# An encoder trunk on one core: adaLN sums moved to VectorE and TensorE, attention's scaling to ScalarE, the first mixer's end in another order

## The chip, the cores and the metric

The kernel runs on one NeuronCore of a Trainium2 chip. The metric is the device time of one execution in microseconds; the median of three runs stands for the kernel. The core's engines run side by side, each through its own queue in order: TensorE (matmuls and transposes), VectorE (DVE), ScalarE (ACT), GpSimd (POOL) and SyncE (SP), which only issues DMAs. Semaphores order them against each other.

## What is computed

Two layers over x of 1024 tokens by 1024 features, all in f32. Each layer has a token mixer and a gated MLP, each of them modulated by a condition vector c.

```python
def adaln(c, w, b):
    mod = (c @ w + b)[:, None, :]
    shift, scale, gate = jnp.split(mod, 3, axis=-1)
# hybrid_mixer(u): a, g, q, k, v = split(u @ w_in)
    h = a * jax.nn.sigmoid(g)
    h = causal_dwconv(h, conv_w, conv_b)                # 31 taps
    h = jax.nn.silu(layer_norm(h, conv_ln_g, conv_ln_b))
    q, k = partial_rotary(q, cos, sin), partial_rotary(k, cos, sin)
    o = swa_sink_attention(q, k, v, sinks)              # softmax with a sink, window of 2 chunks of 64
    return jnp.concatenate([h, o], axis=-1) @ w_out
# per layer
    u = x * (1.0 + scale) + shift
    x = layer_norm(DN_ALPHA * x + (1.0 + gate) * hybrid_mixer(u), ln1_g, ln1_b)
    # then the same with conv_gated_mlp: (val * silu(dwconv3(gate))) @ w_down
```

## The kernel before

**Slabs.** Features lie on partitions. The work is a list of 128-column weight slabs (`SLABS`), each applied to one of two token blocks of 512. A slab is eight k steps (six or five for the MLP's down projection) of three matmuls, since f32 operands are split into a rounded part and a rest: u_hi with w_hi, u_lo with w_hi, u_hi with w_lo (L727 to L729). A slab's weights are loaded into `raw` by SP four slabs ahead, ScalarE rounds them to w_hi (L916) three slabs ahead, and GpSimd subtracts to get w_lo (L1533, four operations per slab). Slabs 0 to 13 are the first block's w_in (convolution's g and a, then q, k, v), 14 to 21 the second block's q and half of its g and a, 22 to 29 the first block's w_out ("o"), 30 to 35 the rest of the second block's w_in, and from 36 on MLP slabs with the other mixers' slabs between them. Slabs 0 and 1, 22 and 23, 36 and 37 run as pairs. Slab 14 begins at about 131.5 us of the trace, 22 at 206.5 (its first matmul later), 24 at 251.6, 36 at 340.2 and 44 at 402.9.

**The plan.** `plan()` hands the other work to slabs as steps. After its part of slab n (evacuating the slab's bank, splitting weights) each engine does its share of `STEPS[n]`, in order. The steps that matter here: "ad" is a quarter of an adaLN chunk (512 of 3072 columns, eight products of a 128x512 tile with a number of c, two in a quarter), for which SP loads 512 KB, ScalarE multiplies (L1039) and GpSimd adds (L1599, L1603); "as" is the chunk's sum over partitions on TensorE (L824); "fold" adds the biases on VectorE. "tap" is a stretch of the convolution's 31 multiply-adds on VectorE (L1236 to L1246), as many as the slab's budget holds (7.6 each, against `early` for slabs 0 to 21 and `room` after them); "cs" is GpSimd's sum over channels. "ro" and "rs" are the rotation: TensorE permutes (L776), VectorE multiplies and later adds (L1323 to L1338), GpSimd multiplies the other half (L1588, L1590); "vt" turns v.

**Attention** goes by beats, one chunk of 64 tokens each: "sc" scores on TensorE (L796), "mx" maxima on VectorE and exponentials on ScalarE (L1347 to L1352, L1016), "pr" the division by the sum on VectorE (L1357 to L1361), "tr" transposes on TensorE (L805) with a copy on ScalarE (L1025), "pv" the product with v on TensorE (L815), then a_hi on ScalarE (L1031) and a_lo on VectorE (L1369). In slabs 14 to 21 a slab holds sc, pr of the chunk before, mx, tr of two before and pv of three before. Slab 21 is `wait`, the last before w_out: all that is left of the first mixer stands there, first the convolution's mean and centring ("cm", "cc"), then the last beats, then its inverse deviation ("cv", "cq", "cr") and swish ("ck", "cn", "cl").

**The prologue.** VectorE builds the first four adaLN chunks alone (`add_first`, 8 operations for each), TensorE sums them over partitions (L846), then gain and bias are folded and u_hi and u_lo of the first block made. GpSimd computes the rotation's angles and then waits for all 32 additions before it splits the first weights.

**x's normalisation.** "xm", "xc", "xv", "xq", "xr", "xk", "xl" are its mean, centring and squares, inverse deviation, scaling and next inputs; GpSimd sums (L1643, L1614). PSUM banks fg0 to fg2 hold slabs, two in turn before slab 36 and three after it.

## Time and profile before

| what | value |
|---|---|
| median of 3 runs | 2229.36 us (2228.52 to 2230.97) |
| profiled execution | 2230.16 us, span 2228.4 us |
| TensorE matmuls | 2125.2 us busy, 95% of the span |
| VectorE, ScalarE, GpSimd | 1183.0, 1010.4, 1422.8 us busy |

The profile's own two lines of TensorE and of its clock, in 40 slices of the span (busy share and granted clock in tenths, 9 is 90% or more):

```profile
PE   5987898999999999999999999999999999999996
...
PEclk9999889999999999999999999999999999999998
```

The first eighth of the span is where TensorE is not full and where its clock falls. A row of the view of stretches, as used below, holds the stretch and its length, then for TensorE (PE), its weight loads (PEld), VectorE, ScalarE and GpSimd the busy us with the count of instructions, then TensorE's granted clock, the DMA engines' busy share and GB/s. No clock was recorded before 47.9 us; that view counts it as full there.

### The profile page before, as it was taken

The numbers are of one execution on the slowest core, as the hardware profiler recorded it, in microseconds if no ns is written. First come the engines' busy times: TensorE is split into PE (matmuls) and PEld (weight loads), VectorE is DVE, ScalarE is ACT, GpSimd is POOL, SyncE is SP. The second block draws the span as 40 slices with busy tenths as digits, with TensorE's granted clock in tenths as the row PEclk, the third lists the DMA queues.
The fourth block names the chain that finished last, engine by engine and source line by source line (L and its number), as shares of the span: only waits on it lengthen the run. The fifth ranks groups of instructions, "written<-read, shape, count | busy, mean of one in ns | idle before, by whom it ended". The sixth has DMA issues, their size and how long they took to land.

```text
span 2228.4 us, 26925 instructions
## 1 busy us (share of the span) xinstructions
PE 2125.2 (95%) x9491; PEld 1719.5 (77%) x9491; DVE 1183.0 (53%) x1916; ACT 1010.4 (45%) x1760; POOL 1422.8 (64%) x1786
## 2 busy tenths in 40 slices
PE   5987898999999999999999999999999999999996
PEld 4865676787888877878778888888778888888885
DVE  6767766666522545567762365467763254332224
ACT  2645444554532656436352565424353364433332
POOL 5886585676566887767556876555555767545452
PEclk9999889999999999999999999999999999999998
DMA  8644342343343334534323432332323333334332
GB/s 281 183 115 123 87 131 85 106 143 101 109 119 104 117 111 141 158 114 136 98 75 104 127 99 82 104 90 79 93 78 98 96 89 92 116 93 135 88 95 73
DMA packets 417283, 248.79 MB, mean 112 GB/s; under 512 B 44309, under 2 KB 389245, under 8 KB 417149
## 3 DMA queue, kind: packets, MB, share of 16 engines
q1 hardware_dynamic: 416282, 246.72, 37.6%
q8 instruction: 76, 1.25, 0.2%
q14 instruction: 58, 0.48, 0.1%
q10 hardware_dynamic: 867, 0.35, 0.1%
HBM read 242.77 MB, written 4.26 MB: 111 GB/s over the span
## 4 chain that ended last, share of the span: by engine, by line
PE 72%; POOL 15%; issue 6%; DVE 4%; ACT 2%; DMA 1%; SPq 1%; DVEq 0%; POOLq 0%; ACTq 0%
PE fg L727 23%; PE fg L729 23%; PE fg L728 23%; POOL w_lo L1533 8%; POOL ada_acc L1603 3%; PE bank_s L796 1%; POOL q L1588 1%; DVE bank_c L1241 1%; POOL ssum L1643 1%; POOL ssum L1614 1%; PE bank_t L815 1%; DMA first_ada<-in_w_ada_mix_dram 1%; PE bank_l L734 0%; PE bank_t L805 0%; POOL ada_acc L1599 0%
## 5 line engine op out<-in xcount | busy, mean ns | idle before, releaser
L1533 POOL TENSOR_TENSOR w_lo<-raw,w_hi 128x256 fp32r<-128x256 f32 (+1 forms) x1440 | 1036.0, 751 | 721.8 <-ACT w_hi L916 717.8
L727 PE MATMUL fg<-u_hi,w_hi 128*128 128x512 f32 x2112 | 853.7, 404 | 8.6 <-DVE u_lo L1290 4.4
L728 PE MATMUL fg<-u_lo,w_hi 128*128 128x512 f32 x2112 | 828.6, 392 | 0.0
L729 PE MATMUL fg<-u_hi,w_lo 128*128 128x512 f32 x2112 | 827.9, 392 | 0.0
L916 ACT ACTIVATE w_hi<-raw 128x1024 fp32r<-128x1024 f32 (+2 forms) x392 | 379.4, 968 | 411.0 <-PE fg L729 332.9
L727 PEld LDWEIGHTS fg<-u_hi,w_hi 128*128 128x128 f32 x2112 | 400.8, 190 | 109.3 <-issue 23.6
L728 PEld LDWEIGHTS fg<-u_lo,w_hi 128*128 128x128 f32 x2112 | 401.0, 190 | 89.9 <-issue 9.7
L729 PEld LDWEIGHTS fg<-u_hi,w_lo 128*128 128x128 f32 x2112 | 400.4, 190 | 85.8
L1455 DVE SCALAR_TENSOR_TENSOR x<-fg,mod,x 128x512 f32<-128x512 f32 x160 | 120.0, 750 | 373.1 <-PE fg L729 373.1
L1241 DVE SCALAR_TENSOR_TENSOR bank_c<-glu,par,bank_c 128x512 f32<-128x512 f32 x448 | 305.5, 747 | 0.0
L727 PE MATMUL fg<-h_hi,w_hi 128*128 128x512 f32 x704 | 281.3, 400 | 1.7 <-DVE h_lo L1488 1.7
L728 PE MATMUL fg<-h_lo,w_hi 128*128 128x512 f32 x704 | 278.4, 395 | 0.0
L729 PE MATMUL fg<-h_hi,w_lo 128*128 128x512 f32 x704 | 278.4, 395 | 0.0
L1465 DVE SCALAR_TENSOR_TENSOR fg<-gate,par,fg 128x512 f32<-128x512 f32 x88 | 66.5, 755 | 362.8 <-ACT fg L1100 362.7
L1603 POOL TENSOR_TENSOR ada_acc<-ada_acc,ada 128x512 f32<-128x512 f32 x120 | 156.4, 1304 | 5.9 <-ACT ada L1039 1.1
L727 PEld LDWEIGHTS fg<-h_hi,w_hi 128*128 128x128 f32 x704 | 132.3, 188 | 34.1 <-DVE h_lo L1488 2.1
L728 PEld LDWEIGHTS fg<-h_lo,w_hi 128*128 128x128 f32 x704 | 132.3, 188 | 32.0 <-issue 1.0
L729 PEld LDWEIGHTS fg<-h_hi,w_lo 128*128 128x128 f32 x704 | 132.3, 188 | 32.0
L1110 ACT ACTIVATE h_hi<-fg 128x512 fp32r<-128x512 f32 x88 | 52.6, 598 | 198.6 <-DVE fg L1481 198.6
L1039 ACT ACTIVATE ada<-ada,ccol 128x512 f32<-128x512 f32 x160 | 106.3, 715 | 12.4 <-DMA ada<-in_w_ada_ffn_dram 12.3
L1481 DVE SCALAR_TENSOR_TENSOR fg<-fg,tanh_c 128x512 f32<-128x512 f32 x88 | 61.4, 698 | 61.7 <-PE fg L729 60.1
L1105 ACT ACTIVATE tanh_c<-fg 128x512 f32<-128x512 f32 x88 | 52.7, 599 | 70.3 <-DVE fg L1468 70.3
(209 smaller groups left out, 1759.4 us busy)
## 6 DMA issues: line engine op xcount, KB each, us to landing
raw<-in_w_up_dram SPq DMA_DIRECT2D x176, 512.0 KB, 3.8
ada<-in_w_ada_ffn_dram SPq DMA_DIRECT2D x48, 512.0 KB, 4.4
raw<-in_w_down_dram SPq DMA_DIRECT2D x64, 384.0 KB, 3.4
raw<-in_w_in_dram SPq DMA_DIRECT2D x40, 512.0 KB, 3.9
raw<-in_w_down_dram SPq DMA_DIRECT2D x64, 320.0 KB, 3.0
ada<-in_w_ada_mix_dram SPq DMA_DIRECT2D x32, 512.0 KB, 4.6
first_ada<-in_w_ada_mix_dram SPq DMA_DIRECT2D x8, 1024.0 KB, 12.6
raw<-in_w_in_dram SPq DMA_DIRECT2D x32, 256.0 KB, 3.7
```

The lines of the kernel that those rows point to most:

```text
L727: pe.matmul(out[:], hi[:, k, :], rhi, start=k == order[0], stop=False)
L728: pe.matmul(out[:], hi[:, k, :], rlo, start=False, stop=False)
L729: ins = pe.matmul(out[:], lo[:, k, :], rhi, start=False, stop=k == order[-1])
L916: act.activation(w_hi[n % NHI][:, 0:nk, :], raw[n % NRAW][:, 0:nk, :], ACT.Copy).then_inc(hi_ready, 1)
L1039: act.activation(ada[m % 2][:, i, :], ada[m % 2][:, i, :], ACT.Copy, scale=ccol[:, k:k + 1]).then_inc(ada_mul, 1)
L1105: act.activation(tanh_c[:], ps[:], ACT.Tanh, scale=0.5).then_inc(gate_act, 1)
L1241: ins = dve.scalar_tensor_tensor(out=conv[:, j, :] if k == CONV_K - 1 else acc[:], in0=src, scalar=w, in1=acc[:], op0=ALU.mult, op1=ALU.add)
L1455: dve.scalar_tensor_tensor(out=xs(b, k), in0=ps[:], scalar=at_gate, in1=xs(b, k), op0=ALU.mult, op1=ALU.add).then_inc(freed["dve"], 1)
L1465: dve.scalar_tensor_tensor(out=ps[:], in0=gate[:, 1:1 + T], scalar=par3[:, l, i + FT:i + FT + 1], in1=ps[:], op0=ALU.mult, op1=ALU.add).th ...
L1481: dve.scalar_tensor_tensor(out=ps[:], in0=ps[:], scalar=0.5, in1=tanh_c[:], op0=ALU.mult, op1=ALU.mult).then_inc(gate_dve, 1)
L1533: ins = pool.tensor_tensor(w_lo[n % NRAW][:, ks, :], raw[n % NRAW][:, ks, :], w_hi[n % NHI][:, ks, :].bitcast(F32), ALU.subtract)
L1603: pool.tensor_tensor(acc[:], acc[:], rows[:, i, :], ALU.add).then_inc(ada_add, 1)
```

## The change

1. `add_first` makes six instead of eight operations per chunk (`ADDED_FIRST`). TensorE multiplies the columns of k = 6 and 7 itself, accumulating in the same bank, and then adds the sums of VectorE's part. The weights of slab 1 are loaded before the last two adaLN loads, and GpSimd no longer waits for the additions before it splits the first weights.
2. Chunks 8, 9 and 10 (`DVE_CHUNKS`) are multiplied and added on VectorE, two operations per quarter; ScalarE and GpSimd leave them out. Chunks 5 to 12 stand beside other slabs than before, none of them beside the two first rotations (slabs 9 to 13 and 37 to 41). Two folds of gates and one of gain and bias move five to seven slabs back.
3. "pr" keeps its two small operations on VectorE; the product with the reciprocals goes to ScalarE as four activations of 128 columns. Its budget falls from 11 to 3.
4. In slabs before 21 VectorE does "pv" after the taps. The budget of slabs 14 to 21 rises from 75 to 80. In the planner's count the first mixer's taps then end in slab 19, its mean and centring stand in slab 20 (`middle`), and in slab 21 the last beats are interleaved with the inverse deviation.
5. GpSimd does its half of the rotation ahead of w_lo in each slab.

```diff
@@ -104,6 +104,7 @@
+LAST_BEAT = POS["o", 0, 0, 0] - 1
...
@@ -155,9 +160,9 @@
-    fixed = {"ro": 14, "mx": 13, "pr": 11, "pv": 5, "cc": 7, "cq": 36, "ck": 7, "cn": 7, "cl": 7, "xc": 7, "xq": 36, "xk": 7,
+    fixed = {"ro": 14, "mx": 13, "pr": 3, "pv": 5, "cc": 7, "cq": 36, "ck": 7, "cn": 7, "cl": 7, "xc": 7, "xq": 36, "xk": 7,
              "xl": 7, "il": 0, "xt": 7, "fold": 8, "hist": 0}
-    early = [62] * 5 + [58] * 4 + [64] * 5 + [75] * (POS["o", 0, 0, 0] - 14)
+    early = [62] * 5 + [58] * 4 + [64] * 5 + [80] * (POS["o", 0, 0, 0] - 14)
@@ -242,14 +247,16 @@
-    quarters = {4: 2, 5: 6, 6: 10, 7: 14, 8: 18, 9: 22, 10: 26, 11: (32, 33, 36, 37), 12: 44, 13: 56, 14: 60, 15: 80, 16: 106,
-                17: 124, 18: 128, 19: 140, 20: 144, 21: 154, 22: 158, 23: 204}
+    quarters = {4: 2, 5: (6, 7, 8, 14), 6: 15, 7: 19, 8: 23, 9: 27, 10: (31, 32, 34, 35), 11: 42, 12: 48, 13: 56, 14: 60, 15: 80,
+                16: 106, 17: 124, 18: 128, 19: 140, 20: 144, 21: 154, 22: 158, 23: 204}
...
+            if c in DVE_CHUNKS:
+                used[n] += 15
         put(ns[-1] + 2, "as", c)
-    for n, what, i in ((12, "gate", 0), (28, "ss", 1), (40, "gate", 1), (100, "ss", 2), (145, "gate", 2), (165, "ss", 3),
+    for n, what, i in ((18, "gate", 0), (33, "ss", 1), (47, "gate", 1), (100, "ss", 2), (145, "gate", 2), (165, "ss", 3),
@@ -273,16 +280,26 @@
-    taps(0, 1, wait)
-    beat(wait, wait - first)
-    put(wait, "cm", 0)
-    for k in range(CT):
-        put(wait, "cc", 0, k)
-    for i in range(wait - first + 1, NCH + 3):
-        beat(wait, i)
-    conv_norm_rest = ("cv", "cq", "cr")
-    for what in conv_norm_rest:
-        put(wait, what, 0)
+    end = taps(0, 1, wait)
+    i = wait - first
+    middle = min(end + 1, wait)
+
+    def norm_first():
+        put(middle, "cm", 0)
+        for k in range(CT):
+            put(middle, "cc", 0, k)
+
+    if middle < wait:
+        norm_first()
+    chunk_step(wait, 0, ("sc", i), ("pr", i - 1), ("mx", i))
+    if middle == wait:
+        norm_first()
+    chunk_step(wait, 0, ("tr", i - 2), ("pv", i - 3))
+    put(wait, "cv", 0)
+    put(wait, "cq", 0)
+    chunk_step(wait, 0, ("tr", i - 1), ("pv", i - 2), ("pr", i))
+    put(wait, "cr", 0)
+    chunk_step(wait, 0, ("tr", i), ("pv", i - 1), ("pv", i))
...
@@ -589,7 +606,7 @@
                 if m >= 2:
-                    sp.wait_ge(ada_add, added(m - 2))
+                    sp.wait_ge(ada_add[added(m - 2)[0]], added(m - 2)[1])
@@ -631,9 +648,9 @@
+            load_w(1)
             load_first(6)
             load_first(7)
-            load_w(1)
@@ -817,7 +834,8 @@
             def sum_ada(c):
-                pe.wait_ge(ada_add, 7 * (c - CHUNKS_BEFORE + 1))
+                e, adds = added((c - CHUNKS_BEFORE + 1) * QUARTERS - 1)
+                pe.wait_ge(ada_add[e], adds)
@@ -840,10 +858,16 @@
+            pe.wait_ge(set_col, 1)
             for c in range(CHUNKS_BEFORE):
-                pe.wait_ge(first_add, DT * (c + 1))
+                pe.wait_ge(in_first[2 * c + 1], 16)
+                for k in range(ADDED_FIRST, DT):
+                    for i in range(TB):
+                        pe.matmul(bank_s[:, c * TB + i:c * TB + i + 1], first_ada[2 * c + 1][:, k % (DT // 2), i * P:(i + 1) * P],
+                                  ccol[:, k:k + 1], start=(c, k, i) == (0, ADDED_FIRST, 0), stop=False)
+                pe.wait_ge(first_add, ADDED_FIRST * (c + 1))
                 for i in range(c * TB, (c + 1) * TB):
-                    ins = pe.matmul(bank_s[:, i:i + 1], first_acc[:, i * P:(i + 1) * P], ones_1[:, 0:1], start=True, stop=True)
+                    ins = pe.matmul(bank_s[:, i:i + 1], first_acc[:, i * P:(i + 1) * P], ones_1[:, 0:1], start=False, stop=i == 2 * DT - 1)
@@ -1016,6 +1040,13 @@
+            def normalise(mi, i):
+                n, r = NCH * mi + i, i % 2
+                act.wait_ge(att_pr, 3 * n + 2)
+                for p in range(QT):
+                    ins = act.activation(probs[:, r, p, :], probs[:, r, p, :], ACT.Copy, scale=st[:, r, 6, p:p + 1])
+                ins.then_inc(att_pr, 1)
@@ -1129,11 +1160,13 @@
+                    elif what == "pr":
+                        normalise(*step[1:])
...
-                    elif what == "ad":
+                    elif what == "ad" and step[1] not in DVE_CHUNKS:
...
@@ -1268,6 +1301,21 @@
+            def add_ada(c, part):
+                m = (c - CHUNKS_BEFORE) * QUARTERS + part
+                rows, acc, n = ada[m % 2], ada_acc[c % 2], added(m)[1]
+                dve.wait_ge(in_ada[m % 2], 16 * (m // 2 + 1))
+                for i in (0, 1):
+                    weight = ccol[:, 2 * part + i:2 * part + i + 1]
+                    if part == 0 and i == 0:
+                        if c >= CHUNKS_BEFORE + 2:
+                            dve.wait_ge(ada_sum, c - CHUNKS_BEFORE)
+                        dve.tensor_scalar(acc[:], rows[:, 0, :], weight, None, ALU.mult).then_inc(ada_add["dve"], 1)
+                    else:
+                        dve.wait_ge(ada_add["dve"], n - 2 + i)
+                        dve.scalar_tensor_tensor(out=acc[:], in0=rows[:, i, :], scalar=weight, in1=acc[:],
+                                                 op0=ALU.mult, op1=ALU.add).then_inc(ada_add["dve"], 1)
@@ -1351,16 +1399,12 @@
-            def normalise(mi, i):
+            def weights(mi, i):
...
-                dve.wait_ge(att_pr, 3 * n + 2)
-                dve.tensor_tensor(probs[:, r, :, :], probs[:, r, :, :],
-                                  st[:, r, 6, :].rearrange("p (i o) -> p i o", o=1).to_broadcast([P, QT, P]),
-                                  ALU.mult).then_inc(att_pr, 1)
...
@@ -1417,7 +1463,7 @@
             for c in range(CHUNKS_BEFORE):
-                for k in range(DT):
+                for k in range(ADDED_FIRST):
@@ -1435,7 +1481,9 @@
-                mine = [step for step in STEPS[n] if step[0] in DVE_STEPS]
+                mine = [step for step in STEPS[n] if step[0] in DVE_STEPS or step[0] == "ad" and step[1] in DVE_CHUNKS]
+                if n < LAST_BEAT:
+                    mine.sort(key=lambda step: step[0] == "pv")
@@ -1592,15 +1640,16 @@
-                pool.wait_ge(ada_mul, 2 * (m + 1))
+                n = added(m)[1]
+                pool.wait_ge(ada_mul, 2 * sum(added(i)[0] == "pool" for i in range(m + 1)))
...
-                    pool.tensor_tensor(acc[:], rows[:, 0, :], rows[:, 1, :], ALU.add).then_inc(ada_add, 1)
+                    pool.tensor_tensor(acc[:], rows[:, 0, :], rows[:, 1, :], ALU.add).then_inc(ada_add["pool"], 1)
                 else:
                     for i in (0, 1):
-                        pool.wait_ge(ada_add, added(m - 1) + i)
-                        pool.tensor_tensor(acc[:], acc[:], rows[:, i, :], ALU.add).then_inc(ada_add, 1)
+                        pool.wait_ge(ada_add["pool"], n - 2 + i)
+                        pool.tensor_tensor(acc[:], acc[:], rows[:, i, :], ALU.add).then_inc(ada_add["pool"], 1)
@@ -1643,9 +1692,9 @@
-            pool.wait_ge(first_add, DT * CHUNKS_BEFORE)
             for n in range(2):
                 split_lo(n)
+            pool.wait_ge(ada_sum, 1)
@@ -1653,6 +1702,9 @@
             for n in range(NSLAB):
+                for step in STEPS[n]:
+                    if step[0] == "ro":
+                        rope(*step[1:])
@@ -1663,9 +1715,7 @@
-                    elif what == "ro":
-                        rope(*step[1:])
-                    elif what == "ad":
+                    elif what == "ad" and step[1] not in DVE_CHUNKS:
@@ -1679,7 +1729,9 @@
 def added(m):
-    return 7 * (m // QUARTERS) + 2 * (m % QUARTERS) + 1
+    engines = ["dve" if CHUNKS_BEFORE + i // QUARTERS in DVE_CHUNKS else "pool" for i in range(m + 1)]
+    e = engines[m]
+    return e, sum(2 - (e == "pool" and i % QUARTERS == 0) for i in range(m + 1) if engines[i] == e)
```

## Rows read from the trace of the kernel before

**Rows 1.** The view of stretches, five between slab boundaries.

```profile
131.50:206.50 75.00, 61.80 (x311) 49.92 (x310) 57.80 (x100) 35.24 (x96) 53.48 (x59) 0.93 0.43 127
206.50:251.60 45.10, 25.97 (x98) 17.23 (x98) 27.03 (x57) 19.38 (x47) 11.27 (x12) 0.70 0.09 24
251.60:340.20 88.60, 78.34 (x326) 62.68 (x324) 63.86 (x102) 44.39 (x65) 77.17 (x86) 0.91 0.49 143
340.20:402.90 62.70, 56.66 (x218) 43.93 (x218) 36.04 (x55) 23.66 (x38) 34.91 (x43) 0.88 0.26 76
402.90:2228.40 1825.50, 1798.84 (x8083) 1460.33 (x8081) 907.71 (x1473) 823.30 (x1419) 1150.46 (x1461) 0.99 0.36 105
```

**Rows 2.** Stretches again: slab 25 (plain), slab 28 and slab 31.

```profile
257.98:263.42 5.44, 5.44 (x25) 4.50 (x24) 5.12 (x8) 3.16 (x5) 5.36 (x6) 1.00 0.67 194
274.30:286.40 12.10, 9.73 (x34) 7.98 (x34) 4.05 (x6) 3.78 (x6) 12.02 (x14) 0.72 0.51 146
297.27:307.44 10.17, 8.18 (x27) 6.13 (x27) 6.08 (x10) 3.93 (x6) 9.29 (x11) 0.83 0.29 93
```

**Rows 3.** TensorE's waits, 44 to 405 us: releaser, us in total, times, longest.

```profile
PE bank_t L786 <- DVE kz L1338: 13.0, 2, 8.4
...
PE bank_l L734 <- POOL ssum L1631: 5.3, 1, 5.3
...
PE bank_l L824 <- POOL ada_acc L1603: 2.7, 2, 2.4
```

**Rows 4.** Timeline of the prologue: start, us, instruction, idle before and its releaser.

```profile
31.51 5.54 DVE L1173 SCALAR_TENSOR_TENSOR first_acc<-first_ada,ccol,first_acc 128x512 f32<-128x512 f32 x7
...
35.22 1.06 ACT L916 ACTIVATE w_hi<-raw 128x1024 fp32r<-128x1024 f32 x1 [8.97 <-DMA raw<-in_w_in_dram]
...
37.11 1.86 PE L846 MATMUL bank_s<-const,first_acc 128*128 128x1 f32 x8 [4.17 <-DVE first_acc L1173]
37.19 6.51 POOL L1533 TENSOR_TENSOR w_lo<-raw,w_hi 128x256 fp32r<-128x256 f32 x8 [3.12 <-issue]
...
41.04 1.21 DVE L1221 TENSOR_TENSOR u_lo<-tmp,u_hi 128x512 fp32r<-128x512 f32 x1
```

**Rows 5.** Timeline at the first mixer's end, VectorE and TensorE.

```profile
214.54 0.68 DVE L1444 SCALAR_TENSOR_TENSOR glu<-tanh_c,fg 128x512 f32<-128x512 f32 x1
...
239.32 1.28 DVE L1303 TENSOR_TENSOR conv<-conv,bank_l 128x512 f32<-128x512 f32 x2 [2.17 <-PE bank_l L742]
...
251.59 0.94 PE L824 MATMUL bank_l<-const,ada_acc 128*128 128x1 f32 x8
```

**Rows 6.** Timeline of TensorE at the first rotation's last two steps.

```profile
134.14 1.10 PE L776 MATMUL bank_t<-probs,const 128*128 128x512 f32 x2 [2.47 <-DVE q L1333]
...
149.24 1.09 PE L786 MATMUL bank_t<-const,v_t 128*128 128x128 f32 x4 [8.38 <-DVE kz L1338]
```

**Rows 7.** Groups of GpSimd's instructions, 252 to 300 us: busy us, mean ns, idle.

```profile
L1533 POOL TENSOR_TENSOR w_lo<-raw,w_hi 128x256 fp32r<-128x256 f32 x32 | 22.6, 743 | 23.5 <-ACT w_hi L916 23.5
L1603 POOL TENSOR_TENSOR ada_acc<-ada_acc,ada 128x512 f32<-128x512 f32 x11 | 14.3, 1296 | 0.4
```

**Rows 8.** Groups of VectorE's instructions, 150 to 207 us (beats of slabs 14 to 21).

```profile
L1241 DVE SCALAR_TENSOR_TENSOR bank_c<-glu,par,bank_c 128x512 f32<-128x512 f32 x34 | 22.9, 747 | 0.0
L1361 DVE TENSOR_TENSOR probs<-probs,st 128x512 f32<-128x512 f32 x6 | 6.2, 1038 | 0.2
...
L1369 DVE TENSOR_TENSOR u_lo<-fg,u_hi 128x256 fp32r<-128x256 f32 x3 | 1.3, 425 | 7.3 <-ACT u_hi L1031 7.3
```

**Rows 9.** Timeline of VectorE: two small operations of one beat.

```profile
161.28 0.17 DVE L1349 SCALAR_TENSOR_TENSOR st<-st,nsink 128x4 f32<-128x4 f32 x1
161.49 0.67 DVE L1352 TENSOR_TENSOR st<-st,nsink 128x4 f32<-128x4 f32 x1
```

**Rows 10.** Timeline of one attention beat of the second mixer, ScalarE and TensorE.

```profile
487.23 0.60 ACT L1110 ACTIVATE h_hi<-fg 128x512 fp32r<-128x512 f32 x1 [1.84 <-DVE fg L1481]
...
487.19 0.60 PE L805 MATMUL bank_t<-const,probs 128*128 128x128 f32 x4
```

12 lines of the change are left out of this document (8 added, 4 removed).

## The prediction

> **What bounds the kernel now.** I read the busy table first. TensorE is busy for 2125.2 of 2228.4 us, so 103 us are idle, and the clock line falls in a few slices of the first fifth and in the last. Next I read the stretches, cut at slab boundaries. From 402.9 us on TensorE is busy 1798.8 of 1825.5 us at a granted clock of 0.99, while each of the four stretches before it loses idle time and clock together [rows 1]. Whatever this change wins must come from the first 403 us. One k step of a slab is three matmuls and a slab of eight steps (24 matmuls) takes 5.44 us at the full clock [rows 2]. That is the floor against which I measure each stretch. The list of waits then names who ends the idle time: the keys of the rotation, and GpSimd's sums for the convolution and for adaLN [rows 3].
>
> **Part 1, first adaLN sums.** VectorE makes six of eight additions per chunk; TensorE takes the products for k = 6 and 7 and later adds the column sums. Now the last seven additions run from 31.51 to 37.05 us with no wait, the four sums follow until 38.97, and the first slab starts at 43.91, as GpSimd's w_lo (eight operations, 6.5 us) is done at 43.7 and had sat idle for 3.1 us until VectorE's last addition [rows 4]. After the change GpSimd doesn't wait: it is free at 34.1, so w_lo is ready near 40.6. The load of slab 1's weights moves ahead of the last two adaLN loads. ScalarE's split of those weights shows their landing, 35.2 [rows 4]; as the same bytes are moved in another order, I take 35.2 for the last adaLN load instead. VectorE needs two more additions (0.79 apart), to 36.8. TensorE needs eight more matmuls of a 128-column weight, 16 records. Eight such records take 1.86 us at the 1.2 GHz level [rows 4], so 16 take 3.7, and with the final 1.9 the sums end at 40.8, 1.8 later than now; at the 2.4 GHz level eight take 0.94 [rows 5], and the end is 38.0, 1.0 earlier. The first u_lo ends 42.2 at most, 3.3 or less after the sums [rows 4], which gives 41 to 44. Near the middle that is 1.4 earlier, and u_lo no longer shares its time with w_lo: I take 2 us saved, with bounds from 4 saved to 1.5 lost.
>
> **Part 2, slabs 14 to 21 (131.5 to 206.5 us, 75.0 us).** Two waits of 2.5 and 8.4 us stand here [rows 6]. Both are GpSimd's half of the rotation: its queue ran late, since each slab cost 3.0 (w_lo, four operations) + 2.6 (adaLN) [rows 7] and two more operations of 128x512 at 1.3 us, for the rotation and the second block's u_lo: 8.2, more than a slab. Now no adaLN part stands beside slabs 9 to 13 and the rotation goes ahead of w_lo: 5.6 us per slab, below the 6.0 of a slab with its rotation (5.44 and 0.5 [rows 2, 6]). The keys then come from VectorE, which has up to 6 additions of the convolution ahead of them (0.67 each [rows 8]), 7 to 9 us after slab 13's end at 131.5, where now TensorE goes on 17.7 after it. Slab 14 ends some 6.4 after slab 13, so 0.5 to 2 us of wait stay. TensorE's own work in the stretch is 61.8 us [rows 1]; 1.9 of it is the half clock that the long wait brings, the convolution's mean adds 1.1 to it, and with 2 of wait that is 63, so 12 saved. Eight slabs in it make a beat of 7.6 us, and this holds if VectorE keeps that pace. Its work in a beat: glu 0.7 (half of them), maxima 1.4, reciprocal 0.4, a_lo 0.4, six or seven additions at 0.67, in all 7.0. The product with the reciprocals (1.04 each) leaves for ScalarE, and the wait for a_hi (7.3 us in three beats) is now behind the additions [rows 8]. ScalarE pays four activations of 128 columns, about 0.27 apart as its exponentials are, 1.1 us, and is busy under half of this stretch [rows 1]. Bounds: 9 to 14 saved.
>
> **Part 3, the end of the first mixer (206.5 to 251.6, 45.1 us).** I follow the chain. VectorE reaches glu of slab 21 only at 214.54, 8.0 us after the slab [rows 5]; with a pace of 7.0 that lag goes. The convolution's additions end in slab 19, so its mean, centring (2.5) and squares run beside slab 21, and the 5.3 us wait for GpSimd's sum [rows 3] goes too. The rest, from slab 21's end: glu and reciprocals 1.2, maxima to 3.0, exponentials to 4.7, t_copy and a_hi to 5.7, a_lo to 6.1, inverse root and diagonals to 9.9, a_lo and reciprocals to 10.7, the weights' scaling on ScalarE to 11.9, transposes and product with v for the last two chunks, with their copies, to 16.5. From there the swish chain is unchanged: from 239.32 to the pair's end at 251.6 is 12 [rows 5]. That is 28.3 us, 17 saved. What is late next is the same alternation of VectorE and ScalarE; nothing else ends later. Bounds: 10 (a lag of half a beat stays and ScalarE's new step sits in the chain twice) to 20.
>
> **Part 4, slabs 24 to 35 (88.6 us).** Twelve slabs are 65.3. GpSimd pays 3.0 for w_lo, 1.3 for the residual sum and 2.6 for adaLN, 6.9 a slab and above 5.44 [rows 7], and TensorE waits for its adaLN sum (2.7 in all [rows 3]) and later for its residual sum; the clock falls each time (0.91 [rows 1]). With chunks 8 to 10 on VectorE, GpSimd has 4.3. Slab 28 with its wait takes 12.1 and slab 31 takes 10.2 [rows 2]; a plain slab with the small matmuls before it is 6.3, so 5.8 and 3.9 can go. The square sums before slab 33 alternate with ScalarE and stay. VectorE takes two additions per part, 1.5 us; with 0.75 for x and three convolution additions (2.0) an output slab holds 4.3. Two things cost: the fold for the second modulation moves from slab 28 to 33, in front of the normalisation's scaling (5 small operations of 0.17 to 0.67 us [rows 9], 0.9 to 3.4, minus about 1 beside TensorE's broadcast), and part 2 of chunk 10 stands in the middle of that scaling (1.5). I take 1.7 lost for both, since VectorE's other operations there run freer: 8 saved. Bounds 3 to 11. Each load of a part is queued on SP behind the weights; it lands 4 to 6 us later. VectorE would wait for it with the next x update behind it, but the banks of an output slab are needed only a slab later, so I cost that at nothing; without that cover it is 2 to 5 us once, after slab 23.
>
> A rule speaks against this part. Small VectorE operations with both inputs in SBUF take 0.17 us at one time and 0.67 right after [rows 9], when GpSimd is busy, while the convolution's additions, one of whose inputs is in PSUM, stay at 0.747 [rows 8]. The Trainium skill ("SBUF — State Buffer", Who interferes with whom) says that a VectorE instruction with two SBUF inputs locks GpSimd's reads out for its length. The new additions are of that kind. By that rule 24 of them could each hold GpSimd for 0.75 us, 18 us of its time over 13 slabs; with it GpSimd has 4.3 + 1.4, 0.3 above a slab, some 3 us late by the end and within the low bound.
>
> **Part 5, slabs 36 to 43 (62.7 us).** The wait for the keys comes again, 13.0 - 8.4 = 4.6 us [rows 3, 6], and the queries' sums are late before it; TensorE is busy 56.7 of 62.7 us, of which about 3.2 are lost to the clock (0.88) [rows 1]. With the rotation ahead of w_lo, which here waits for ScalarE, and chunk 11 moved to slabs 42 to 45, GpSimd's half is done 2.2 us after the rotation. The floor is 56.7 - 3.2 = 53.5. Saved 9, bounds 5 to 11.
>
> **Part 6, from 402.9 us.** One adaLN sum of 0.8 moves into this stretch. In the attention beats of mixers 1 to 3 the scaling sits on ScalarE ahead of a_hi. Now ScalarE is idle for 1.84 us behind a_hi, until 487.2, which is when the transposes that need a_hi's bank start, at 487.19 [rows 10]. With 1.1 us more, a_lo is done near 487.0: just in time in beats with an adaLN part. Mixer 1's additions end four slabs later (they yield to the adaLN parts), so its normalisation falls on three more beats. I take 2 us lost, bounds from 1 gained to 8 lost.
>
> **Sum.** 2 + 12 + 17 + 8 + 9 - 2 = 46. The profiled execution took 2230.2 us (span 2228.4, 1.8 around it), which gives 2184.2; the median of the runs is 2229.4, 0.8 below it, so the forecast is 2183.4.
>
> **The rivals.** (a) VectorE stays the bound in slabs 14 to 21: small operations at 0.67 beside GpSimd and seven additions instead of six make a beat of 8.5 or more. For it: the beats now lengthen from 7.6 to 10. Against it: 1.04 plus 2.4 of waiting leave every beat. Then part 2 gives 8, part 3 gives 8, the rest stays: 46 - 13 = 33, 2196; with part 4 at its low end, 28, 2201. (b) More than forecast: the waits' end keeps the clock at 2.4 GHz throughout the four stretches, and the sums of the prologue run at it. Lost to clock now in 131.5 to 402.9: roughly 0.07x75, 0.09x89 and 0.12x63, 21 us, of which I have counted about 9; so up to 12 more, 2171. By the Trainium skill ("TensorE: Matmul & The Clock Gate", What's actually happening) activity releases the throttle; the trace agrees, as the clock falls only around the waits named. (c) Slower than before: ScalarE, with 1.1 us more, becomes late in every one of the 24 attention beats of mixers 1 to 3, so that the transposes wait for bank_t. Place: the second slab of each pair. It tells from the first delay beyond the slack of [rows 10]; to cancel 46 us each beat must lose 1.9, and at 2.4 the time is 2241. Against it: ScalarE is 45% busy there. (d) The change does nothing where the idle time is, because another wait takes over in each stretch (the loads, for one): 2229.
>
> **Chances.** Forecast 0.70, with its own range 2174 to 2197; (a) 0.14; (b) 0.11; (c) 0.03; (d) 0.02. The range 2170 to 2202 takes in (a) and (b) and leaves out part of the tails of each, (c) and (d). A measurement of this kernel tells 0.2%, 4.5 us, from no change: faster 0.95, same 0.02, slower 0.03.
>
> **What would show it.** Right: in the list of waits the keys (13.0) fall below 3, GpSimd's adaLN sum and the convolution sum vanish, slab 21 ends near 192, the output pair near 220, and the stretch from slab 44 on keeps its 1825 us within 3. Part 1 is wrong if the first slab starts after 43.9; part 2 if VectorE's glu of slab 21 comes more than 2 us after the slab; part 3 if the pair's end is over 33 us after slab 21; part 4 if VectorE sits idle for adaLN loads with TensorE waiting behind it. The prediction as a whole is wrong if the attention beats after 403 us show waits for ScalarE over 10 us, or if the clock still falls in as many places as now.

## The result, and the profile after

| what | before | after |
|---|---|---|
| median (lowest to highest of 4) | 2229.47 us (2228.52 to 2230.97) | 2189.45 us (2187.96 to 2193.33) |
| ratio, 95% interval | 1 | 0.9822 (0.981 to 0.9834) |
| profiled execution | 2230.16, span 2228.4 | 2193.33, span 2190.8 |

The change saves 40.0 us, 1.8%, against a forecast of 46. The profiled execution of after is the longest of its four, 3.9 above the median, so its stretches add up to 37.6 saved. Below, single stretches are compared in profiles and totals by medians; where the two disagree, the text gives both. The page's two lines of TensorE after:

```profile
PE   7998989999999999999999999999999999999996
...
PEclk9998989999999999999999999999999999999998
```

The view of stretches, at the same slab boundaries as [rows 1] (columns as there):

```profile
131.58:196.62 65.04, 62.36 (x313) 49.66 (x312) 56.80 (x98) 44.69 (x133) 44.64 (x52) 0.97 0.43 130
196.62:228.76 32.14, 23.42 (x95) 15.65 (x93) 17.04 (x41) 17.62 (x42) 7.78 (x8) 0.73 0.11 33
228.76:312.69 83.93, 74.90 (x326) 60.70 (x325) 69.12 (x107) 32.67 (x47) 64.92 (x70) 0.94 0.55 169
312.69:364.59 51.90, 51.58 (x218) 40.71 (x219) 35.53 (x55) 22.44 (x36) 30.84 (x39) 0.97 0.28 82
364.59:2190.80 1826.21, 1798.69 (x8091) 1460.41 (x8089) 891.55 (x1469) 853.91 (x1522) 1148.11 (x1469) 1.00 0.36 106
```

| stretch | before | after | saved | forecast |
|---|---|---|---|---|
| to slab 13's end | 131.5 | 131.6 | -0.1 | 2 |
| slabs 14 to 21 | 75.0 | 65.0 | 10.0 | 12 |
| end of the first mixer | 45.1 | 32.1 | 13.0 | 17 |
| slabs 24 to 35 | 88.6 | 83.9 | 4.7 | 8 |
| slabs 36 to 43 | 62.7 | 51.9 | 10.8 | 9 |
| the rest | 1825.5 | 1826.2 | -0.7 | -2 |

TensorE's waits after, 44 to 400 us (releaser, us in total, times, longest):

```profile
PE fg L744 <- DVE u_lo L1338: 5.4, 1, 5.4
PE fg L832 <- DVE u_lo L1413: 3.5, 2, 1.9
PE bank_l L759 <- DVE diag L1302: 3.1, 1, 3.1
PE bank_l L755 <- POOL ssum L1663: 2.8, 1, 2.8
...
PE bank_l L755 <- POOL ssum L1670: 0.8, 1, 0.8
PE bank_t L803 <- ACT q L1111: 0.7, 1, 0.7
```

Against [rows 3], the keys (13.0) and the adaLN sums (2.7) are gone and the convolution's sum is down from 5.3 to 0.8. Most of what is left belongs to two chains that no step of the change shortens: inverse root and diagonals at the mixer's end (3.1; before 3.6 in two waits), and x's normalisation before slabs 33 (2.8; before 1.3) and 36 (5.4; before 4.4). The wait of 1.9 in the second line is new. Slab 21 ends at 196.6 and the pair at 228.8, where I had 192 and 220.

The prologue after, as a timeline:

```profile
31.84 7.93 POOL L1581 TENSOR_TENSOR w_lo<-raw,w_hi 128x256 fp32r<-128x256 f32 x8
...
37.05 3.57 PE L866 MATMUL bank_s<-ccol,first_ada 128*128 128x1 f32 x16 [1.43 <-DMA first_ada<-in_w_ada_mix_dram]
40.48 1.84 PE L870 MATMUL bank_s<-const,first_acc 128*128 128x1 f32 x8
...
44.11 0.67 DVE L1254 TENSOR_TENSOR u_lo<-tmp,u_hi 128x512 fp32r<-128x512 f32 x1
...
44.93 0.76 PE L744 MATMUL fg<-u_hi,w_hi 128*128 128x512 f32 x1 [1.86 <-DVE u_lo L1254]
```

GpSimd is early, as forecast, and u_lo takes 0.67 instead of the 1.21 of [rows 4]. But the last adaLN load lands at 37.05, and TensorE's products and sums stand behind it: the first slab starts at 44.93, 1.0 later than before. By slab 13's end all but 0.1 of that is made up.

### The profile page after: what moved, and what is told of

It is laid out like the page before. It is cut to its first block, busy times and chain, and to the rows that moved or that the text cites. A ratio compares the mean times of both kernels' runs of the same rounds, so it can differ in the third digit from the quotient of the medians.

```text
span 2190.8 us, 27121 instructions
## 1 busy us (share of the span) xinstructions
PE 2127.2 (97%) x9555; PEld 1725.9 (79%) x9555; DVE 1161.0 (53%) x1900; ACT 1031.0 (47%) x1864; POOL 1391.3 (64%) x1765
## 3 DMA queue, kind: packets, MB, share of 16 engines
q8 instruction: 76, 1.25, 0.2%
## 4 chain that ended last, share of the span: by engine, by line
PE 83%; POOL 5%; DVE 4%; ACT 3%; issue 3%; SPq 1%; DMA 1%; DVEq 0%; POOLq 0%; ACTq 0%
PE fg L744 26%; PE fg L746 26%; PE fg L745 26%; POOL w_lo L1581 2%; DVE bank_c L1274 1%; PE bank_s L813 1%; POOL ssum L1663 1%; POOL ada_acc L1652 1%; ACT ada L1070 1%; DMA first_ada<-in_w_ada_mix_dram 1%; PE bank_t L832 1%; SPq L602 1%; PE bank_t L793 0%; PE bank_l L842 0%; PE bank_l L751 0%
## 5 line engine op out<-in xcount | busy, mean ns | idle before, releaser
L1652 POOL TENSOR_TENSOR ada_acc<-ada_acc,ada 128x512 f32<-128x512 f32 x102 | 132.2, 1296 | 4.5 <-ACT ada L1070 0.5
L1070 ACT ACTIVATE ada<-ada,ccol 128x512 f32<-128x512 f32 x136 | 90.3, 714 | 3.6 <-DMA ada<-in_w_ada_mix_dram 2.6
```

The lines of the kernel that those rows point to most:

```text
L1070: act.activation(ada[m % 2][:, i, :], ada[m % 2][:, i, :], ACT.Copy, scale=ccol[:, k:k + 1]).then_inc(ada_mul, 1)
L1652: pool.tensor_tensor(acc[:], acc[:], rows[:, i, :], ALU.add).then_inc(ada_add["pool"], 1)
```

## The experiments

All are edits of the changed kernel ("after"), with its stretches as the yardstick: first slab at 44.9, then 65.0, 32.1, 83.9 and 51.9 us. How far a stretch moves by itself can be read where an edit doesn't touch it. With after's own prologue, seven other kernels start the first slab at 44.4 to 45.2. With after's own steps at the mixer's end, that stretch took 32.1 at a granted clock of 0.73 in after, 32.1 at 0.73 with chunks 8 to 10 back on GpSimd, 30.4 at 0.78 with slab 1's weights loaded last, and 30.2 at 0.83 with chunk 10 later. Slabs 24 to 35 took 83.9 in after and 82.5 with slab 1's weights loaded last. So a difference under 2 us in either of these two stretches says little.

**The prologue, three ways.** Without TensorE's share:

```diff
-ADDED_FIRST = 6
+ADDED_FIRST = DT
...
```

> The changed kernel with one part undone: VectorE makes all eight additions of each first adaLN chunk again and TensorE only the column sums; the freed GpSimd and the new order of loads stay. In the changed kernel the last adaLN load landed at 37.0 us, the sums ended at 42.3 and the first slab started at 44.93. Theory A: what costs in part 1 is TensorE's share behind the last load (16 matmul records, 3.6 us at the 1.2 GHz level). Then VectorE, with two more additions behind the last load (0.79 each at best, 1.1 as they were recorded beside GpSimd), is done near 39 and the sums near 41: the first slab starts at 43 to 44, 1 to 2 us earlier than in the changed kernel, and the whole is 0 to 2 us shorter. Theory B: VectorE, with GpSimd's w_lo beside it, is the bound: six or eight additions more at 1.1 us each put its end at 40.5 or later, the first slab starts at 45 to 46, and the share of TensorE has saved about 1 us after all. Everything behind the first slab keeps its lengths within 1 us.

Median 2192.3 (ratio 0.9829, 0.9814 to 0.9843); first slab 44.64. Neither theory's figure came. VectorE's seven additions, and GpSimd's work beside them:

```profile
32.87 7.19 DVE L1206 SCALAR_TENSOR_TENSOR first_acc<-first_ada,ccol,first_acc 128x512 f32<-128x512 f32 x7
33.94 8.07 POOL L1581 TENSOR_TENSOR w_lo<-raw,w_hi 128x256 fp32r<-128x256 f32 x8
```

They take 1.03 us each, not the 0.79 of [rows 4] (the five that run wholly beside w_lo about 1.09); that puts the sums' end at 42.0, beside 42.3 with TensorE's share. But the two executions don't compare as they stand: here the last adaLN load was there at 35.3 (issued at 24.1, 11.2 to landing), in after at 37.05, with the same order of loads. With a landing at 37.05, four additions behind it and the last sums would end near 43.5 (estimate from the durations above), 1.2 later than after's. The next kernel says the same.

With slab 1's weights loaded last:

```diff
             load_first(5)
-            load_w(1)
             load_first(6)
             load_first(7)
+            load_w(1)
```

> The changed kernel with the weights of slab 1 loaded behind the last two adaLN loads, as before. My estimate was that the last adaLN load would land at 35.2 us; it landed at 37.0. Theory A (bytes in another order): with the old order of loads the last adaLN load lands near 35.2, the sums end 1.5 to 1.8 us earlier (40.5) and the first slab, a pair with slab 1, starts at 43 if slab 1's weights (landing near 37, split on ScalarE and GpSimd in some 4 us) are ready by then, or stays at 44 to 45 if they are not. Theory B (the queue isn't the limit; landing times are set by the other transfers under way): the last adaLN load lands at 36.5 to 37 in both orders and slab 1's weights come later, so the first slab starts 1 to 3 us later than in the changed kernel (46 to 48).

Median 2189.48 (0.9822, 0.9806 to 0.9839); first slab 43.38, 1.55 earlier. Theory A. TensorE's timeline, where the columns' sums end at 40.78, as my step had them (40.8):

```profile
35.53 3.55 PE L866 MATMUL bank_s<-ccol,first_ada 128*128 128x1 f32 x16
...
38.94 1.84 PE L870 MATMUL bank_s<-const,first_acc 128*128 128x1 f32 x8
```

Its last load was there at 35.03, nearly as in the kernel without TensorE's share, and its sums end 1.3 earlier than that one's 42.04: TensorE's share is worth some 1.2 us, the saving that theory B had named. The order of loads itself: in the ten kernels with the new order the last adaLN load landed at 35.3 to 37.3, in the three changed kernels with the old one at 33.5, 33.7 and 35.0. The total hardly moves beside after's median of 2189.45; the four executions spread over 3.1 us, so a gain of 1.5 doesn't show there.

With GpSimd waiting for the additions again:

```diff
             angles()
+            pool.wait_ge(first_add, ADDED_FIRST * CHUNKS_BEFORE)
             for n in range(2):
```

> The changed kernel, but GpSimd waits again for VectorE's first adaLN additions before it makes the w_lo of the first two slabs. It prices the sharing of SBUF by itself. In the changed kernel VectorE's last five additions took 5.62 us (1.12 each) while w_lo ran beside them; before, alone, they started 0.79 apart. Theory A (the two slow each other): without w_lo beside them the last five take 4.0 us, the sums end 0 to 1.5 us earlier if the additions and not the last load set the end, and w_lo takes 6.5 instead of 7.9 us; but it starts only at about 38, ends near 44.5 and the first u_lo, which then shares its time with w_lo again, puts the first slab at 45 to 47: 0 to 2 us later than the changed kernel. Theory B (no contention; the additions only waited for loads): the additions keep 5.6 us and w_lo its 7.9.

Median 2189.72 (0.9825, 0.981 to 0.9839); first slab 46.13, 1.2 later, as theory A has it, although the last load landed 0.6 earlier than in after (36.4). With nothing beside them, both engines are faster:

```profile
36.42 1.54 DVE L1206 SCALAR_TENSOR_TENSOR first_acc<-first_ada,ccol,first_acc 128x512 f32<-128x512 f32 x2 [1.17 <-DMA first_ada<-in_w_ada_mix_dram]
...
38.10 5.69 POOL L1581 TENSOR_TENSOR w_lo<-raw,w_hi 128x256 fp32r<-128x256 f32 x8 [6.51 <-issue]
```

**The scaling back on VectorE.**

```diff
-                    elif what == "pr":
-                        normalise(*step[1:])
...
+                dve.tensor_tensor(probs[:, r, :, :], probs[:, r, :, :],
+                                  st[:, r, 6, :].rearrange("p (i o) -> p i o", o=1).to_broadcast([P, QT, P]),
+                                  ALU.mult).then_inc(att_pr, 1)
```

> The changed kernel with the probabilities scaled on VectorE again (one operation of 1.04 us per beat in place of four activations on ScalarE), nothing else moved. Theory A (VectorE's pace sets slabs 14 to 21): its beat, 7.0 by my count, becomes 8.0 to 8.2, so each of the seven beats with a scaling costs 0.8 to 1.1 us: the stretch from slab 13's end to slab 21's end (65.0 us in the changed kernel) becomes 69 to 73, and the first mixer's end 1 us longer besides; the whole is 5 to 9 us longer. Theory B (what sets those slabs is GpSimd's rotation at their start, and VectorE has room): 65 to 67, the whole within 3 us of the changed kernel. Behind 403 us, where ScalarE gives the time back, both expect the same length within 2 us.

Median 2195.86 (0.9849, 0.9834 to 0.9864), 6.4 longer than after, within theory A's 5 to 9. Slabs 14 to 21:

```profile
131.33:199.76 68.43, 62.60 (x313) 49.65 (x312) 63.90 (x104) 36.67 (x107) 45.75 (x51) 0.98 0.41 124
```

3.4 more than 65.0, a little under theory A's 69, and 0.6 more at the mixer's end (32.7 at a clock of 0.79; with after's steps and slab 1's weights loaded last it was 30.4 at 0.78). Behind slab 44 nothing changes (0.4 shorter).

**a_lo ahead of the additions.**

```diff
-                if n < LAST_BEAT:
-                    mine.sort(key=lambda step: step[0] == "pv")
```

> The changed kernel without VectorE's a_lo moved behind its convolution additions in the first mixer's slabs. In the changed kernel TensorE waited 1.9 us at 171.75 for this a_lo and its clock fell for 3.4 us. Theory A (the move saves more than this wait costs): with a_lo ahead of the additions VectorE waits 2 to 3 us in each of five or more beats for a_hi, as before (7.3 us in three beats), and the stretch to slab 21's end grows from 65.0 to 70 or more. Theory B (with the scaling on ScalarE, a_hi comes early enough and the move is not needed): 62 to 65 us, as the wait at 171.75 goes, and the whole is 0 to 3 us shorter than the changed kernel.

Median 2196.49 (0.9847, 0.9831 to 0.9862). The stretch takes 69.5:

```profile
131.56:201.05 69.49, 62.57 (x313) 49.30 (x312) 55.00 (x98) 44.36 (x131) 44.23 (x52) 0.98 0.40 122
```

Theory A, a little under its 70: the order of two steps is worth 4.5 us, more than moving the scaling. The medians differ by 7.0.

**GpSimd's rotation behind w_lo.**

```diff
-                for step in STEPS[n]:
-                    if step[0] == "ro":
-                        rope(*step[1:])
                 if n + NHI < NSLAB:
                     split_lo(n + NHI)
...
+                    elif what == "ro":
+                        rope(*step[1:])
```

> The changed kernel with GpSimd's half of the rotation behind the w_lo of its slab again, as before. Theory A (this order is what took away the two waits for the keys): at slab 13 the keys come 2.8 us later and at slabs 37 to 41 by as much plus what w_lo waits there for ScalarE, so a wait of 3 to 6 us stands at one or both places and the clock falls there: the whole is 5 to 12 us longer. Theory B (the adaLN parts moved away from the rotations did it alone: GpSimd then has 5.6 us a slab either way): 0 to 2 us longer.

Median 2199.84 (0.9862, 0.9846 to 0.9877), 10.4 longer: theory A. TensorE waits for the keys again, 6.1 in all; the stretches of slabs 14 to 21 and 36 to 43:

```profile
130.80:198.13 67.33, 62.31 (x313) 49.65 (x312) 60.12 (x102) 44.68 (x133) 44.55 (x52) 0.97 0.42 126
310.97:369.32 58.35, 53.97 (x218) 42.58 (x219) 35.07 (x54) 22.35 (x36) 30.46 (x39) 0.91 0.25 73
```

2.3 and 6.4 more. Between them this execution was 3.2 shorter, and its clock was halved for a shorter time there.

**The mixer's end in the old order.**

```diff
-    end = taps(0, 1, wait)
...
+    taps(0, 1, wait)
+    beat(wait, wait - first)
+    put(wait, "cm", 0)
...
+    for i in range(wait - first + 1, NCH + 3):
+        beat(wait, i)
+    for what in ("cv", "cq", "cr"):
+        put(wait, what, 0)
```

> The changed kernel with the end of the first mixer in the old order: the convolution's mean, centring, variance and scaling behind whole beats, not between them. In the changed kernel the pair ended 32.1 us after slab 21; before, 45.1, of which 8.0 was VectorE's lag behind slab 21. Theory A (the reordering is what saved most): the lag is gone anyway (-8), the rest comes back, and the pair ends 37 to 40 us after slab 21, the whole 5 to 8 us longer than the changed kernel. Theory B (the lag and the scaling on ScalarE were all): 32 to 34 us, the whole within 2.

Median 2194.56 (0.9834, 0.9817 to 0.9852).

```profile
131.22:193.55 62.33, 59.65 (x311) 48.12 (x310) 54.67 (x94) 43.35 (x129) 43.25 (x51) 1.00 0.45 136
193.55:230.22 36.67, 24.15 (x97) 16.01 (x95) 18.69 (x45) 19.32 (x44) 9.07 (x9) 0.72 0.10 29
```

The end takes 36.7, just below theory A's 37, and 4.5 more than after's. But the slabs before it take 2.7 less. The centring no longer stands among them, and the clock isn't halved there, though the wait that after has at 171.75 is there too:

```profile
171.35 0.65 PE L821 MATMUL fg<-probs_t,v 128*64 128x256 f32 x4 [1.90 <-DVE u_lo L1402]
```

With after's steps and an unbroken clock these slabs take 63.4 (the fillers' kernel, below), so some 1.6 of the 2.7 is the clock and 1.1 the centring. In the profiles the new order saves 1.8 us net; without the clock's part it would be 3.4 (estimate), and the medians say 5.1, theory A's lower edge. Each is the smaller part of the 22.9 that the two stretches saved.

**Another order of my own:** variance and inverse root ahead of the last transposes, swish between the last attention steps.

```diff
-    chunk_step(wait, 0, ("tr", i - 2), ("pv", i - 3))
     put(wait, "cv", 0)
     put(wait, "cq", 0)
-    chunk_step(wait, 0, ("tr", i - 1), ("pv", i - 2), ("pr", i))
+    chunk_step(wait, 0, ("tr", i - 2), ("pv", i - 3), ("tr", i - 1), ("pr", i), ("pv", i - 2))
     put(wait, "cr", 0)
...
```

> The changed kernel with another order at the first mixer's end: the convolution's variance, its inverse root and its diagonals come ahead of the transposes for chunks 5 and 6 on all engines, and the first steps of the swish chain stand between the last attention steps. In the changed kernel VectorE waited 2.6 us for a_hi ahead of the inverse root (202.80) and 4.5 us ahead of a_lo(6), while chunk 7's reciprocal, whose exponentials were done at 202.0, came at 207.9. Theory A (the end is a chain of VectorE's own order, with room in it): the inverse root starts near 200.6, chunk 7's weights near 205, its a_lo near 211 instead of 214.8, and the swish chain, begun near 208 instead of 215, ends near 219. The pair starts at 210 to 212, and ends 26 to 30 us after slab 21 instead of 32.1. Theory B (a chain through ScalarE's copies and TensorE's product with v, which the order doesn't shorten): 31 to 33 us.

Median 2193.1 (0.9835, 0.982 to 0.985). The end takes 35.2 us, worse than both theories. The waits say why:

```profile
PE fg L838 <- DVE u_lo L1419: 7.0, 4, 2.7
...
PE fg L750 <- DVE u_lo L1419: 2.3, 1, 2.3
```

a_lo(4) now sits behind the inverse root on VectorE, and TensorE's product for chunk 5 needs the bank that it frees; that pushes ScalarE's copies behind chunk 7's scaling. Theory A had taken VectorE's order as the chain. Theory B named ScalarE's copies and TensorE's product, but held that the order doesn't matter; the chain goes through all three, and the order made it longer.

**Chunks 8 to 10 back on ScalarE and GpSimd,** at their new places.

```diff
-DVE_CHUNKS = (8, 9, 10)
+DVE_CHUNKS = ()
...
-            if c in DVE_CHUNKS:
+            if c in (8, 9, 10):
```

> The changed kernel with adaLN chunks 8 to 10 back on ScalarE (products) and GpSimd (sums), at the places and with the planner's costs that they have now. In the changed kernel the stretch from the output pair's end to slab 36's start took 83.9 us, against 88.6 before and 80.6 by my forecast. Theory A (GpSimd is the bound of slabs 24 to 35 and VectorE's share relieves it): GpSimd pays 6.9 us per output slab again, TensorE waits for adaLN or residual sums, and the stretch becomes 86 to 89. Theory B (the 3.2 us missing from my forecast is what VectorE's additions cost GpSimd and the normalisation's chain): without them w_lo falls from 3.4-3.7 back to 2.8 us a slab and the square sums from 9.5 to 8.5 us, and the stretch is 82 to 85. The stretches before the pair keep their lengths within 1 us.

Median 2203.76 (0.9877, 0.9862 to 0.9893), 14.3 longer, the largest difference of all.

```profile
227.83:323.38 95.55, 77.45 (x325) 62.08 (x325) 52.45 (x85) 47.00 (x69) 81.55 (x89) 0.92 0.49 144
```

Theory A's direction, above its 89: TensorE waits 2.7 for an adaLN sum, 2.2 for the mean's sum, 5.6 for the squares' and 6.7 before slab 36. The new places, two parts beside the squares, are affordable only on VectorE.

**Chunk 10 later, and one product fewer for TensorE.**

```diff
-ADDED_FIRST = 6
+ADDED_FIRST = 7
...
-    quarters = {4: 2, 5: (6, 7, 8, 14), 6: 15, 7: 19, 8: 23, 9: 27, 10: (31, 32, 34, 35), 11: 42, 12: 48, 13: 56, 14: 60, 15: 80,
+    quarters = {4: 2, 5: (6, 7, 8, 14), 6: 15, 7: 19, 8: 23, 9: 27, 10: 36, 11: 42, 12: 48, 13: 56, 14: 60, 15: 80,
```

and slab 1's weights loaded last.

> The changed kernel with two edits that are read in separate stretches. First, TensorE takes only the products for k = 7 of the first adaLN sums, and slab 1's weights are loaded last: with the loads in that order TensorE's share had ended 2 us behind VectorE's additions (37.0), so one product less for TensorE and one addition more for VectorE should balance them: the sums end near 39.9 instead of 40.8, and the first slab starts at 42.4 to 42.8 (44.93 in the changed kernel, 43.38 with the loads alone). If TensorE's share isn't what sets the end, it stays at 43.4. Second, chunk 10's additions go from slabs 31, 32, 34 and 35 to slabs 36 to 39, away from the normalisation's square sums and scaling. Theory A (these additions, by the sharing of SBUF and by their place in the chain, are what the stretch from the pair's end to slab 36's start is longer by than I forecast, 83.9 instead of 80.6): the square sums on GpSimd take 8.5 us again instead of 9.5, the wait before the variance sum falls from 2.8 to 1.8 or less, the wait before slab 36 from 5.4 to 4, and the stretch is 80.5 to 82. Theory B (the chain of the normalisation with the fold in front of it is the whole of it): 83 to 84. In both, slabs 36 to 43 lose 0 to 2 us to the moved additions.

Median 2188.39 (0.981, 0.9795 to 0.9824). First slab at 43.04, 0.3 better than with the loads alone and short of 42.8. The stretch of slabs 24 to 35 takes 81.8, within theory A, but the loads alone already gave 82.5 there (their granted clock 0.96 in it, here 0.98, after 0.94), so 0.6 at most is this edit's; slabs 36 to 43 lose 0.4. The wait before the variance's sum falls from 2.8 to 1.8, as theory A has it, but the one before slab 36 rises from 5.4 to 6.2, where it had 4. The squares' sums on GpSimd, after's first, this kernel's second:

```profile
276.33 9.46 POOL L1663 TENSOR_TENSOR ssum<-tmp,ssum 128x512 f32<-128x512 f32 x6 [0.80 <-ACT tmp L975]
```

```profile
272.50 8.45 POOL L1663 TENSOR_TENSOR ssum<-tmp,ssum 128x512 f32<-128x512 f32 x6 [0.80 <-ACT tmp L975]
```

So VectorE's additions do cost GpSimd 1.0 us there. The other 1.5, the part inside the scaling, was hidden: without it VectorE waits 1.50 us for ScalarE at the same place.

**Fillers on TensorE.**

The kernel has 66 matmuls of 128x512 whose results nobody reads: 32 at the first mixer's end, 12 ahead of the variance's sum before slab 33, 22 ahead of slab 36.

```diff
...
+            def fill(count, n):
+                pe.wait_ge(lo_ready, n + 1)
+                pe.wait_ge(*freeing(PREV[n]))
+                for i in range(count):
+                    pe.matmul(fg[BANK[n]][:], w_hi[n % NHI][:, i % DT, :], u_hi[1][:, i % DT, :], start=True, stop=True)
...
```

> The changed kernel with matmuls of 128x512 whose results nobody reads where TensorE waits: 8, 12, 7 and 5 at the first mixer's end, 12 ahead of the variance's sum before slab 33, and 22 ahead of slab 36. Each takes 0.227 us at the 2.4 GHz level, 0.43 at the 1.2 GHz level. They price the half clock behind waits. In the changed kernel the clock was halved in 203.5 to 220.6, 285.4 to 292.3 and 309.3 to 316.2, and the output pair took 13.4 us, slab 33 took 7.8 and the pair of slab 36 took 12.6, where 10.9, 5.4 and 10.9 are the full-clock times. Theory A (the pair's end is set by TensorE at half clock, not by the swish chain as I forecast): with the clock kept, the pair takes 11 to 11.5 and the stretch from slab 21's end to the pair's end 28 to 30 instead of 32.1; the stretch to slab 36's start becomes 80 to 82, and slabs 36 to 43 lose another 1.5: the whole is 5 to 8 us shorter. Theory B (the swish chain, done at 224.9, sets the pair's end, and the fillers delay what waits behind them): the pair's end moves by less than 1 us and the whole by less than 2, or it is longer.

Median 2186.6 (0.9806, 0.9789 to 0.9822), 2.9 less than after, short of theory A's 5 to 8; the profiles differ by 6.8, for after's is a long one. Its stretches:

```profile
130.58:194.02 63.44, 60.72 (x313) 48.53 (x312) 57.13 (x98) 44.75 (x132) 44.59 (x52) 1.00 0.44 133
194.02:223.45 29.43, 27.51 (x127) 19.97 (x125) 17.26 (x41) 17.83 (x42) 7.82 (x8) 0.94 0.12 36
223.45:306.07 82.62, 80.02 (x360) 64.41 (x359) 71.19 (x107) 32.69 (x47) 64.98 (x70) 1.00 0.56 172
306.07:356.35 50.28, 49.95 (x218) 39.52 (x219) 35.54 (x55) 22.45 (x36) 30.82 (x39) 1.00 0.29 85
```

Theory A for the mixer's end: 2.7 shorter. In slabs 24 to 35 it is 1.3 less than after, not the 2 to 4 expected, and no less than the 82.5 that the kernel with slab 1's weights loaded last took without fillers: no gain is shown there. That the faster slabs only reach the next wait sooner would explain it, and isn't shown either.

**All of it together.** The edits of chunk 10's kernel, the fillers (3 instead of 5 ahead of the pair), and 7 more in slab 18.

> What the runs before pointed to, together: slab 1's weights loaded last and seven additions per first chunk on VectorE; chunk 10's additions in slabs 36 to 39; fillers on TensorE (8, 12, 7 and 3 at the first mixer's end, 12 ahead of the variance's sum before slab 33, 22 ahead of slab 36, and 7 new ones in slab 18, ahead of the product with v that waited 1.9 us at 171.75). If the causes are independent, as my theory has it, the gains against the changed kernel's profiled execution add up: 1.9 at the first slab's start, up to 1.6 in slabs 14 to 21, 2.7 at the mixer's end, 1.3 to 3 in slabs 24 to 35, 1.3 in slabs 36 to 43, less about 1.5 lost behind: 7 to 10 us, a span of 2181 to 2184 and a median of 2180 to 2184. The rival: the place of a halved clock depends on waits further ahead, so that what one edit wins another gives back, and the median stays at 2185 to 2188, as with the fillers alone (2186.6).

Median 2184.19 of five executions (0.9794, 0.978 to 0.9807), span 2182.4: below both kernels and 5.3 us under after, at the upper edge of what independent causes would give and under the rival's 2185. The stretches are 63.4, 29.5, 82.6 and 50.3. Chunk 10's move brings nothing there: the squares are summed at 278.67, but twelve fillers, sized for the later sum, hold TensorE until 279.72.

## Why the prediction was right or wrong

The sign, the range and the main causes held: the waits named are gone, and VectorE's glu of slab 21 comes at 196.83, 0.2 after the slab, so rival (a) isn't what happened; the clock falls in four places before slab 44 instead of eight, so neither is (b). Of the six terms, four were too large by 2 to 4 us; two were too cautious, by 1.8 and 1.3, so the total came nearer than most of its terms. Rival (b)'s sum of what the clock costs left out the end of the first mixer, where the granted clock was lowest (0.70 over 45.1 us), and that is where a term for it was missed most.

**Part 1 failed,** by its own test (44.93 against 43.9). The step at fault is "I take 35.2 for the last adaLN load": a load of 512 KB was put ahead of it and it landed at 37.05, and undoing that alone gives 1.55 back (1.0 to 1.8 against the kernels with after's prologue). Why the landing differs by up to 2 us between kernels with the same order stays open. Of the two ends that I worked out, only the one at the 1.2 GHz level came: 3.57 and 1.84 behind the load. The other two steps of the part paid off: GpSimd's freedom is worth 1.2 at least, TensorE's share some 1.2.

**Part 2 was right in its parts.** Undone one by one, the rotation's order costs 2.3, the scaling 3.4, the order of a_lo 4.5; I hadn't given the last a term. ScalarE's four activations take 1.28 us a beat where I counted 1.1: the 0.27 that I took for the distance of two exponentials is that from an exponential to the read of its sum, and two exponentials stand 0.35 apart. The forecast of 63 for the stretch is what two executions with a full clock gave (63.4). After's has one fall of the clock, in slab 19, which takes 7.2 us:

```profile
168.26 1.16 PE L813 MATMUL bank_s<-kz,q 128*128 128x128 f32 x8
169.25 0.60 PE L822 MATMUL bank_t<-const,probs 128*128 128x128 f32 x4
171.75 0.65 PE L832 MATMUL fg<-probs_t,v 128*64 128x256 f32 x4 [1.90 <-DVE u_lo L1413]
```

I priced the move of a_lo at nothing; it makes this wait, which the kernel without the move doesn't have.

**Part 3: mechanism right, one step misnamed.** The lag is gone. "From there the swish chain is unchanged ... 12" treated the tail as VectorE's and ScalarE's. But the last u_lo is ready at 224.9, and the pair ends at 228.8: it takes 13.43 us at a granted clock of 0.80. With fillers it takes 11.52 at 1.00 and the whole end 29.4, against my 28.3:

```profile
215.33:228.76 13.43, 13.43 (x48) 10.73 (x48) 7.99 (x13) 8.07 (x13) 0.00 (x0) 0.80 0.00 0
```

So 2.7 of the missing 3.8 us is the clock that the waits bring. The kernels without fillers agree: the same steps took 32.1, 30.4 and 30.2 at clocks of 0.73, 0.78 and 0.83. The rest, 1.1, lies before the pair. Candidates are two adaLN products of ScalarE (1.32 us at 198.05) ahead of chunk 7's exponentials, and one small operation of VectorE's inverse root that takes 1.25 us at 203.53; no run takes either out.

**Part 4: a gain counted that the next chain took back.** I added 5.8 at slab 28 and 3.9 at slab 31. The variance's sum can't start until the mean has been subtracted, squared and summed by three engines. Mean and variance on TensorE, before and then after:

```profile
299.42 1.12 PE L734 MATMUL bank_l<-ssum,const 128*128 128x512 f32 x2 [1.99 <-POOL ssum L1643]
...
315.29 1.05 PE L738 MATMUL bank_l<-const,ssum 128*128 128x1 f32 x8 [1.29 <-POOL ssum L1614]
```

```profile
270.23 1.12 PE L751 MATMUL bank_l<-ssum,const 128*128 128x512 f32 x2 [0.45 <-POOL ssum L1692]
...
285.84 1.87 PE L755 MATMUL bank_l<-const,ssum 128*128 128x1 f32 x8 [2.79 <-POOL ssum L1663]
```

15.87 and 15.61 apart: that stretch didn't get shorter, although slab 31 itself went from 7.5 to 5.9 us. From the pair's end to the mean 47.8 became 41.5, 6.4 saved; behind the variance 1.9 were lost (24.9 to 26.85), near my 1.7. With 0.3 that gives the 4.7. The rule of the Trainium skill that I weighed ("SBUF — State Buffer", Who interferes with whom) was borne out in direction: w_lo rose from 744 ns, with the sums on GpSimd, to 886 ns (36 operations of slabs 24 to 31), 5 us of GpSimd's time. The only place where a wait of TensorE is seen to shrink without chunk 10's additions is at the squares, from 2.8 to 1.8. VectorE did wait for the loads (5.1 us in all) without TensorE waiting behind it.

**Part 5** saved 1.8 more than forecast: the wait for the keys, 4.6 of the 13.0, fell to nothing and the clock rose from 0.88 to 0.97. **Part 6** was right: the rest lengthened by 0.7, TensorE waits for ScalarE's copies 2.4 us in all there, and with the scaling back on VectorE the rest is the same within 0.4, which settles rival (c).

What stays open: undoing a part costs 2.4 to 5 us more by the medians than by its stretches (6.4 against 4.0 for the scaling, 7.0 against 4.5 for a_lo, 10.4 against 5.5 for the rotation, counting its two stretches less the 3.2 between), most of it because after's profiled execution is the long one; where that one lost its 3.9 us isn't known. Nor is how much of after's spread (5.4 us in four executions; 1.3 with the fillers) is the clock's. Its falls differ between kernels whose waits are alike; I can't say what decides.

## What to carry to other kernels

Follow each stretch by its own chain: a wait removed ahead of a chain of other engines comes back as a wait at its end. Give the clock that a wait brings its own term, read from the slab behind it. Before a load is moved forward, count whose landing it pushes back, and undo parts one at a time: here two lines that sort one engine's steps were worth more than moving the scaling to another engine. Before two executions are compared, look whether the loads landed alike in both; and take the noise of a stretch from the runs that didn't touch it.
